# Stick-breaking attention scores on one Trainium2 core: the second score matmul with 128 rows (64 of them zeros) in place of 64, and key counts in steps of 128 in place of 256

## The reference

```python
Q_BLOCK = 128
def block(args):
    qb, t0 = args
    t = t0 + jnp.arange(Q_BLOCK)
    mask = key_pos[None, :] < t[:, None]
    z = jnp.einsum("bhqd,bhkd->bhqk", qb, kf) * scale
    log_keep = jnp.where(mask, jax.nn.log_sigmoid(-z), 0.0)
    later = lax.cumsum(log_keep, axis=3, reverse=True) - log_keep
    log_a = jax.nn.log_sigmoid(z) + later
    a = jnp.where(mask, jnp.exp(log_a), 0.0)
    return jnp.einsum("bhqk,bhkd->bhqd", a, vf)
```

## Time and profile before

| | |
|---|---|
| median of 3 runs | 2965.73 us (2963.91 to 2967.29) |
| profiled execution: span | 2961.6 us |
| PE busy | 2855.1 us, 96% |
| PE weight loads busy | 2318.3 us, 78% |
| DVE busy | 1471.6 us, 50% |
| ACT busy | 900.8 us, 30% |
| POOL busy | 306.8 us, 10% |
| mean granted TensorE clock | 0.981 |
| stick-breaking stage, first score row to last | 1424.8 to 2077.5 us |

### The profile page before, as it was taken

How to read it: one execution, slowest core, us unless ns; L and a number is a source line. 1 busy time by engine, 2 the same in 40 slices (tenths; PEclk the granted TensorE clock), 3 DMA queues, 4 the chain that set the end, 5 groups by cost and what they waited for, 6 DMA issues and landing times.

```text
span 2961.6 us, 35214 instructions
## 1 busy us (share of the span) xinstructions
PE 2855.1 (96%) x13224; PEld 2318.3 (78%) x13224; DVE 1471.6 (50%) x1842; ACT 900.8 (30%) x1369; POOL 306.8 (10%) x267
## 2 busy tenths in 40 slices
PE   7999999999999999999999999997899999999999
PEld 7888888888888888878766667665788888888887
DVE  6454344344444444365676676676415444444444
ACT  6441112321111111146555555554304111111110
POOL 2200000100000000030233333332002000000000
PEclk9999999999999999999999999997899999999999
DMA  6311111111111111122100000001311111111111
GB/s 209 119 30 56 50 43 50 43 43 57 50 42 50 50 50 42 50 65 99 47 22 28 28 28 21 20 28 59 114 49 44 49 50 42 55 46 48 43 57 64
DMA packets 41855, 158.37 MB, mean 53 GB/s; under 512 B 5552, under 2 KB 5552, under 8 KB 41392
## 3 DMA queue, kind: packets, MB, share of 16 engines
q1 hardware_dynamic: 34704, 124.83, 13.1%
q0 software_dynamic: 6784, 26.22, 2.6%
q10 hardware_dynamic: 288, 6.29, 0.5%
HBM read 138.98 MB, written 18.35 MB: 53 GB/s over the span
## 4 chain that ended last, share of the span: by engine, by line
PE 87%; issue 4%; DVE 3%; POOL 3%; ACT 2%; DMA 0%; POOLq 0%; SPq 0%; ACTq 0%; DVEq 0%
PE ps L1353 26%; PE ps L1355 25%; PE ps L1354 25%; PE ps L1581 3%; PE ps L1624 2%; POOL sig L476 2%; PE ps L1580 2%; PE ps L1583 1%; ACT sig L696 1%; DVE w_lo L860 1%; DVE keep L1092 1%; PE ps L1638 1%; PE ps L1454 1%; PE ps L1483 0%; ACT keep L695 0%
## 5 line engine op out<-in xcount | busy, mean ns | idle before, releaser
L1353 PE MATMUL ps<-xg_hi,w_hi 128*128 128x512 f32 x2560 | 1012.3, 395 | 11.2 <-DVE xg_lo L1209 4.9
L1355 PE MATMUL ps<-xg_hi,w_lo 128*128 128x512 f32 x2560 | 1002.1, 391 | 0.0
L1354 PE MATMUL ps<-xg_lo,w_hi 128*128 128x512 f32 x2560 | 1001.6, 391 | 0.0
L1353 PEld LDWEIGHTS ps<-xg_hi,w_hi 128*128 128x128 f32 x2560 | 483.8, 189 | 109.5 <-issue 6.9
L1355 PEld LDWEIGHTS ps<-xg_hi,w_lo 128*128 128x128 f32 x2560 | 483.4, 189 | 103.6
L1354 PEld LDWEIGHTS ps<-xg_lo,w_hi 128*128 128x128 f32 x2560 | 484.2, 189 | 94.9 <-issue 0.7
L519 ACT ACTIVATE w_hi<-raw 128x1024 fp32r<-128x1024 f32 x228 | 237.9, 1053 | 973.0 <-PE ps L1355 968.5
L860 DVE TENSOR_TENSOR w_lo<-raw,w_hi 128x1024 fp32r<-128x1024 f32 x228 | 290.0, 1279 | 300.8 <-ACT w_hi L519 296.9
L1291 DVE TENSOR_TENSOR x<-x,ps 128x512 f32<-128x512 f32 x352 | 235.5, 685 | 165.3 <-PE ps L1355 164.5
L1353 PE MATMUL ps<-act_hi,w_hi 128*128 128x512 f32 x704 | 277.3, 394 | 2.4 <-DVE x L1291 2.4
L1355 PE MATMUL ps<-act_hi,w_lo 128*128 128x512 f32 x704 | 276.0, 392 | 0.0
(11 more groups left out here) (173 smaller groups left out, 2891.2 us busy)
## 6 DMA issues: line engine op xcount, KB each, us to landing
raw<-wpack SPq DMA_DIRECT2D x228, 512.0 KB, 3.5
x<-xT POOLq DMA_DIRECT2D x2, 2048.0 KB, 13.2
d_x<-x POOLq DMA_DIRECT2D x1, 4096.0 KB, 18.6
x<-d_x ACTq DMA_DIRECT2D x1, 4096.0 KB, 18.3
out<-x SPq DMA_DIRECT2D x8, 512.0 KB, 2.6
d_mix<-o_sum POOLq DMA_DIRECT2D x56, 64.0 KB, 2.0
mx<-d_mix POOLq DMA_DIRECT2D x1, 3584.0 KB, 12.4
d_me<-me_f POOLq DMA_DIRECT2D x4, 512.0 KB, 2.9
```

The lines of the kernel that those rows point to most:

```text
L1353: pe.matmul(out, whi, mhi, start=start, stop=False)
L1354: pe.matmul(out, whi, mlo, start=False, stop=False)
L1355: return pe.matmul(out, wlo, mhi, start=False, stop=stop)
```

## The change

1. The keys' low parts get 128 rows. `sk_lo` was one tile whose 64 rows of a head were used for both parities of the pair; now there are three tiles, one for each slot of `sk`. 64 rows of each hold the low parts, the other 64 zeros, written once by three memsets on DVE in front of pair 0 (`zeros_made`). The second score matmul uses all 128 rows of `sq` and of `sk_lo`; the rows of low query parts meet zeros.
2. The count of keys goes in steps of 128: row r = 0 has 128 keys fewer (n = 256·t + 128), in `z`, in both sigmoids, in the scan and in the product. The mask is 128 columns for both rows.
3. Of the last chunk of an item three blocks are transposed in place of four, its split on ACT and DVE has 384 columns in place of 512, and the last two `weighted` matmuls have 128 columns in place of 256, into the half of the bank that belongs to r = 1.

```diff
@@ places
-        sk_lo = place("sk_lo", [P, 2, SEQ], F32R, Z + 24 * K1)
+        sk_lo = [place("sk_lo0", [P, SEQ], F32R, Z + 24 * K1), place("sk_lo1", [P, SEQ], F32R, Z + 28 * K1),
+                 place("sk_lo2", [P, SEQ], F32R, ME + 11 * K1)]
@@ helpers
+        def key_count(r, t):
+            return 2 * P * t + (r + 1) * P
+        def chunk_cols(t, c):
+            return 3 * P if c == t else 4 * P
@@ POOL weigh, ACT sigmoids, DVE scan, PE z
-                        n = 2 * P * (t + 1)
+                        n = key_count(r, t)
@@ ACT chunk (DVE chunk alike)
-                        act.activation(aT_hi[:, n % 2].rearrange("p a c -> p (a c)"), ps[:, 4 + n % 2, :],
+                        act.activation(aT_hi[:, n % 2].rearrange("p a c -> p (a c)")[:, 0:w], ps[:, 4 + n % 2, 0:w],
@@ DVE, in front of pair 0
                         project(0, piece, piece)
+                        if piece == 2:
+                            dve.memset(fp(sk_lo[0][SHEAD:P, :]), 0.0).then_inc(zeros_made, 1)
+                            dve.memset(fp(sk_lo[1][0:SHEAD, :]), 0.0).then_inc(zeros_made, 1)
...
                         values(0, 0, n, 6 + n)
+                    dve.wait_ge(me_stored, 16 * MHEADS)
+                    dve.memset(fp(sk_lo[2][0:SHEAD, :]), 0.0).then_inc(zeros_made, 1)
@@ PE z
-                        slot, hd, _ = head_place(hh, par)
+                        slot = head_place(hh, par)[0]
...
-                            pe.matmul(o[:, 0:w], sq[hd, slot, q], sk_lo[hd, par, c:c + w], start=False, stop=not final)
-                        m = (2 - r) * P
-                        pe.matmul(o[:, w - m:w], ident_r[:], mask_r[:, 0:m], start=False, stop=True
-                                  ).then_inc(z_full, 1)
+                            pe.matmul(o[:, 0:w], sq[:, slot, q], sk_lo[slot][:, c:c + w], start=False, stop=not final)
+                        pe.matmul(o[:, w - P:w], ident_r[:], mask_r[:], start=False, stop=True).then_inc(z_full, 1)
@@ PE turn
-                        for kk in range(2):
-                            for r in range(2):
-                                k = 2 * c + kk
-                                last = pe.transpose(ps[:, 4 + n % 2, (2 * kk + r) * P:(2 * kk + r + 1) * P],
-                                                    sig[:, it % 2, r, k * P:(k + 1) * P], ident[:])
+                        at = ((0, 0), (0, 1), (1, 1)) if c == it % 4 else ((0, 0), (0, 1), (1, 0), (1, 1))
+                        for j, (kk, r) in enumerate(at):
+                            k = 2 * c + kk
+                            last = pe.transpose(ps[:, 4 + n % 2, j * P:(j + 1) * P],
+                                                sig[:, it % 2, r, k * P:(k + 1) * P], ident[:])
@@ PE weighted
-                            o = ps[:, 6, 0:2 * P]
-                            pe.matmul(o, v, aT_hi[:, n % 2, kk, :], start=(c == 0 and kk == 0), stop=False)
-                            last = pe.matmul(o, v, aT_lo[:, n % 2, kk, :], start=False, stop=(c == t and kk == 1))
+                            edge = c == t and kk == 1
+                            o = ps[:, 6, P:2 * P] if edge else ps[:, 6, 0:2 * P]
+                            cols = slice(0, P) if edge else slice(0, 2 * P)
+                            pe.matmul(o, v, aT_hi[:, n % 2, kk, cols], start=(c == 0 and kk == 0), stop=False)
+                            last = pe.matmul(o, v, aT_lo[:, n % 2, kk, cols], start=False, stop=edge)
```

More of the change, by code:

```diff
@@ L127, in trunk @@
         ident_r = place("ident_r", [P, P], F32R)
-        mask_r = place("mask_r", [P, 2 * P], F32R)
+        mask_r = place("mask_r", [P, P], F32R)
         mean_all = place("mean_all", [P, P], F32)
@@ L167, in trunk @@
         mrt = place("mrt", [P, NMEM], F32, Z + 65 * K1)
-        mask_f = place("mask_f", [P, 2 * P], F32, Z + 66 * K1)
+        mask_f = place("mask_f", [P, P], F32, Z + 66 * K1)
         q_hi = place("q_hi", [P, 2, SEQ], F32R, Z)
@@ L310, in trunk @@
         sqk_lo_ready = sem("sqk_lo_ready")
+        zeros_made = sem("zeros_made")
         vT_full = sem("vT_full")
@@ L417, in _ @@
             pool.affine_select(out=mask_f[:], in_=mask_f[:], compare_op=ALU.is_ge,
-                               fill=0.0, base=0, pattern=[[1, 2 * P]], channel_multiplier=-1
+                               fill=0.0, base=0, pattern=[[1, P]], channel_multiplier=-1
                                ).then_inc(ident_steps, 1)
@@ L715, in chunk @@
                     def chunk(hp, it, c, first):
-                        n = CHUNKS_BEFORE[it] + c
+                        n, w = CHUNKS_BEFORE[it] + c, chunk_cols(it % 4, c)
                         act.wait_ge(aT_full, hp * CHUNKS + (n + 1))
@@ L1118, in lo_part @@
                             hi, lo = ((sq[rows, slot, half], sq[twin, slot, half]),
-                                      (sk[rows, slot, half], sk_lo[rows, to, half]))[part]
+                                      (sk[rows, slot, half], sk_lo[slot][rows, half]))[part]
                             dve.wait_ge(sqk_hi_ready, hp * 12 + ((2, 4)[part] * piece - 4 * part + hh + 1))
@@ L1150, in pair @@
                                 for r in range(2):
-                                    row, n = hp * ROWS + (2 * (it + 1) + r), 2 * P * ((it + 1) % 4 + 1)
+                                    row, n = hp * ROWS + (2 * (it + 1) + r), key_count(r, (it + 1) % 4)
                                     scan(row, (it + 1) % 2, r, (it + 1) % 4)
@@ L1657, in pair @@
                                 turn(hp, it, c, par, first)
+                            if it == ITEMS - 1 and first:
+                                pe.wait_ge(zeros_made, 3)
                             if it == ITEMS - 1 and not last:
@@ L1682, in _ @@
                             pe.wait_ge(sqk_hi_ready, 12)
+                            pe.wait_ge(zeros_made, 2)
                             for r in range(2):
```

8 lines of the change are left out of this document (4 added, 4 removed).

## The result

The changed kernel takes 2881.07 us (median of 4 runs, 2876.96 to 2882.65) against 2965.18 us, ratio 0.9715 (95% interval 0.9701 to 0.9728): 84 us, 2.8% faster. The forecast was 2885. The profiled execution's span fell from 2961.6 to 2881.0 us, by 80.6 us.

The account below looks back on a forecast made before the run. TensorE, busy 96%, was taken as the bound, with 0.20 us lost per row switch. Terms 76.8 + 3.5 + 5.1 − 1.5 − 2 − 1 − 1 + 0.7 = 80.6 us gave 2885 us, range 2868 to 2924.

Parts of the forecast that it names:

- Cost of a switch, 0.20 us: Score rows on the PE: each change between 128 and 64 rows costs 0.20 us; 384 of them make 76.8 us.
- the drain does not go with the 64 rows: Rival: the stall belongs to operands or bank, so only columns and transposes gain, 2958 us; chance 0.05.
- Time taken out of the score rows comes out of the item: Score rows precede the chain to POOL's product and the transposes, so their saving, 76.8 us from switches, shortens every item.
- half of it is hidden: Rival: DVE's back-to-back scans and tf set every item, so r = 1 rows bring nothing, 2923 us; chance 0.14.
- Shorter r = 0 work on ACT, DVE, POOL: Scan, keep and product of r = 0 get shorter, but r = 1 carries the chain in steady pairs: 0 us.
- Transposes, 5.1 us: One transpose fewer an item, 0.106 us each; 48 of 64 counted, the rest in slack: 5.1 us gained.
- The wait for tf: Items scoring t = 2: the projection's wait for DVE's tf grows about 0.4 us, mostly covered by POOL's wait: −1.5 us.
- Items that score t = 0, −2 us: DVE's weight preparation precedes the third chunk and the PE, 0.8 us sooner, nearly catches it: 14 · 0.14, 2 us lost.
- Back edges: Two loop back edges: DVE's 2.60 us stand sets the item, hiding 0.9 us of score rows; 0.5 returns: 1 us lost.
- Prologue −1: Memsets of zeros in DVE's order before the low parts and pair 0: 1 us lost, upper bound 3.7.
- Last pair +0.7: Last pair: hidden r = 1 rows −2, shorter r = 0 work +2.7, low-clock switches +2, lower clock −2: 0.7 us gained.
- The clock (third rival): Rival: new waits drop the granted clock to 1.2 GHz in steady pairs; all 56 items give 3031 us; chance 0.03.

Follow-up runs that it names:

- banks grouped: The kernel before with two-bank score rows ordered high, high, low, low, mask in place of high, low, high, low, mask: 2945.09 us, ratio 0.9938.
- the padding and the short product: Changed kernel with the old key counts, transposes and weighted matmuls, POOL's r = 0 product cut to one column (work left out): 2891.92 us, ratio 0.9744 to the kernel before.

## Why the prediction came out as it did

- **Total: right, but the exact hit is luck.** 80.6 us were forecast and 80.6 measured by the profiled execution, 84 by the medians. A steady pair was to lose (76.8 + 3.5 + 5.1)/8 = 10.7 us less some 0.5 that comes back; it lost 9.7. By the same sums the four steady pairs lost 2 us less than forecast, pair 0 2.6 less, the two pairs behind a back edge 4.8 more, the last pair 1.5 more, and the rest of the program 1.7 less. The pair is 80.99 us long, not the 82 of the stretch in the earlier trace rows, so "pairs of about 71.5" (71.29 measured) was helped by that too.
- **Cost of a switch, 0.20 us: right.** A t = 2 row with four switches is 0.79 us shorter with the padding alone (1.93 to 1.14), banks grouped saves 0.19 per switch, the "issue" rows are gone. Nothing is seen for the extra 64 rows. The second reading of the 76.8 us by the "issue" waits was no independent proof: it adds up 273 waits of 0.28 us on average, not 384 of 0.20. The rival "the drain does not go with the 64 rows" is out, and with it the reading by which padding wins nothing.
- **"Time taken out of the score rows comes out of the item": holds for t = 1, and for t = 0 in the first head, not for t = 2 and 3.** The padding alone realises 6.3 of 9.6 us a pair. That is the part of the rival "half of it is hidden" that came true: DVE's scan r = 0, tf and scan r = 1 stand back to back, and moving the rows together puts POOL's first product beside the second scan. With that product cut, a pair is at 72.4 us, 8.6 below the kernel before (which was not run with the cut itself).
- **"Shorter r = 0 work on ACT, DVE, POOL: in the steady pairs r = 1 carries the chain, so 0": wrong, this is the term that failed.** The key counts are worth 2.5 us a pair alone and 3.4 on top of the padding; columns and transposes were sized at 1.1. The shorter r = 0 scan and product end earlier, which frees DVE for tf and the r = 1 scan from its neighbour on POOL (2.22 us in place of 2.74 with 768 keys). How much of the surplus each of these makes was not separated. This surplus of 2.3 us a pair and the 3.3 missing in the point above cancel for the most part.
- **Matmuls of 128 columns in place of 256, 0:** right, 0.11 us from load to load, and the t = 2 row is only 0.02 us shorter than with the padding alone. That narrow ones would be slow did not happen. Where 512 columns became 384 the row is 0.11 us shorter (1.36 to 1.25), as sized.
- **Transposes, 5.1 us:** 6.3 by the medians, 3.5 by the steady pair; in the intervals with t = 2 they are hidden, as argued, and in those with t = 3 as well, which was not.
- **The wait for tf: grown by 0.4 as forecast** (0.36 to 0.73 us), 8 us over the stage. In the t = 2 item of the first head the PE still has 0.34 us of slack behind it, so there it lies wholly under the wait for POOL. The term of −1.5 us itself was not measured.
- **Items that score t = 0, −2 us:** not seen in the changed kernel, whose two such intervals lost 1.16 and 1.06 us, more than their four switches; with the padding alone the second head gave back half (0.40 of 0.80), with `w_lo` at 1.47 us.
- **Back edges: the sign was wrong.** 1 us of loss was forecast for two; pairs 3 and 5 lost 2.4 us more than a steady one, since the low clock behind the stall was less: over pair 3 the mean granted clock is 1.00 (0.96 before), over pair 5 0.98 (0.94 before). The item with t = 2 takes 8.79 us in pair 3 as in any other pair, 12.81 before; in pair 5 9.93, 13.61 before. Whether the change brings this is not shown.
- **Prologue −1:** 0.5 us for the first two memsets. Pair 0 gained 2 us less than a steady pair, in its first item, where three projection steps take 3.7 us (1439.94 to 1443.66) in place of 2.1, at a granted clock of 0.54, behind a wait of 0.76 us. The item takes 8.1 to 9.7 us in the kernels padded in both heads and 8.5 in the others; whether the change causes it is left open.
- **Last pair +0.7:** 12.9 us measured with its end, 11.4 forecast; the same kernel's second profile has 2 us less again there, so the clock's share can't be told.
- **The clock (third rival)** stayed at 1.00 in the steady pairs.

## What to carry to other kernels

Look at the starts of matmuls, not at their busy time: a load that starts together with its matmul and sits behind "issue" marked a change of the row count here. Padding with zeros took that away for the price of a memset, and putting matmuls of one height together took away half of it in the score rows of two banks for nothing. When a critical chain passes through two score rows, work on the row that is not on the chain can still count, if it shares an engine or overlaps an engine's neighbour on the chain; test the parts of a change alone, since a right sum can hide two wrong terms. Once an item is bound by a chain, moving independent steps behind the last link of it is worth a try, item by item; look at what the link that now comes sooner will run beside.

## What the runs showed of the hardware beyond that

- A scan of 768 keys on DVE takes 1.76 us alone, and with POOL's product already running beside its first 0.46, 0.61 or 1.12 us it takes 2.07, 2.22 or 2.74; of 1024 keys 2.29 alone, 2.75 with 0.61 us of overlap, 3.50 with 1.35. `w_lo` on DVE (128x1024) goes from 1.22 to 2.04 us.
- A switch between 128 and 64 rows costs 0.20 us at a granted clock of 1.00; at 0.50 the interval with 512 columns is 0.72 in place of 0.43 us, so 0.29.
- The granted clock behind a stall of the PE differs between kernels that are nearly the same: behind the same back edge one item took 12.8 us in the kernel before (mean clock of the pair 0.96) and 8.8 in the changed one (1.00).
- Behind the loop's back edge the PE stands 4.9 us put down to "issue" in pair 5 with the padding alone, 5.3 and 5.0 us in pairs 3 and 5 with the padding and the short product; in the changed kernel it is DVE that stands, for 2.4 us. Why one or the other is left open.
